# Scores of the delta-rule chunks without the masked-off half of the early queries, and one weight split per head pair moved to GpSimd

## The reference, cut to what matters

```python
def step(S, inp):
    r_t, w_t, k_t, v_t, aa_t, bb_t = inp
    sa = jnp.einsum('bhvk,bhk->bhv', S, aa_t)
    S = S * w_t[:, :, None, :] + sa[..., None] * bb_t[:, :, None, :] + v_t[..., None] * k_t[:, :, None, :]
    y_t = jnp.einsum('bhvk,bhk->bhv', S, r_t)
    return S, y_t
```

## Time and profile before

| | |
|---|---|
| three timed runs | 1025.52 us median, 1024.86 to 1025.6 |
| the profiled execution | 1025.08 us, its span 1023.1 us |
| TensorE busy | 1010.8 us (99%) |
| DVE busy | 736.5 us (72%) |
| ScalarE busy | 516.5 us (50%) |
| GpSimd busy | 218.1 us (21%) |
| where the changed stages lie | 214 to 540 us of the span |

### The profile page before, as it was taken

The page is one execution under the profiler, slowest core; times in us unless marked ns, Lnnn a source line. Parts: engine busy times, 40 slices in busy tenths (PEclk is TensorE's granted clock), DMA queues, the critical chain, the costliest instruction groups (busy, mean ns, idle before and its releaser), DMA issues.

```text
span 1023.1 us, 18706 instructions
## 1 busy us (share of the span) xinstructions
PE 1010.8 (99%) x7098; PEld 806.0 (79%) x7098; DVE 736.5 (72%) x1233; ACT 516.5 (50%) x869; POOL 218.1 (21%) x290
## 2 busy tenths in 40 slices
PE   8999999999999999999999999999999999999997
PEld 7888888777777777777777888888888888888886
DVE  5224667788988988888877455367777777789786
ACT  6435766844445445345453322265455444467744
POOL 8532356230221312313210454000000000000000
PEclk9999999999999999999999999999999999999999
DMA  7874465331303313214356877613333333337653
GB/s 201 240 218 139 130 215 203 92 77 42 87 24 73 87 63 86 56 63 119 95 161 149 242 233 255 204 37 102 88 103 90 96 101 103 90 115 221 207 186 117
DMA packets 161291, 133.25 MB, mean 130 GB/s; under 512 B 32730, under 2 KB 137736, under 8 KB 161224
## 3 DMA queue, kind: packets, MB, share of 16 engines
q1 hardware_dynamic: 147552, 88.37, 29.8%
q0 software_dynamic: 13520, 43.90, 13.9%
q10 hardware_dynamic: 151, 0.04, 0.0%
HBM read 111.83 MB, written 20.45 MB: 129 GB/s over the span
## 4 chain that ended last, share of the span: by engine, by line
PE 94%; DVE 2%; ACT 1%; issue 1%; DMA 1%; POOL 0%; ACTq 0%; POOLq 0%; DVEq 0%
PE ps L2075 15%; PE ps L2078 14%; PE ps L2077 14%; PE ps L2031 6%; PE ps L2033 5%; PE ps L2032 5%; PE ps L2634 3%; PE ps L2632 3%; PE ps L2633 3%; PE ps L2247 3%; PE ps L2380 2%; PE ps L2188 2%; PE ps L2567 1%; PE ps L2568 1%; PE ps L2566 1%; PE ps L2329 1%
## 5 line engine op out<-in xcount | busy, mean ns | idle before, releaser
L1340 DVE TENSOR_TENSOR wlo<-raw,whi 128x1024 fp32r<-128x1024 f32 x106 | 138.8, 1310 | 131.6 <-ACT whi L874 113.7
L874 ACT ACTIVATE whi<-raw 128x1024 fp32r<-128x1024 f32 x116 | 122.6, 1057 | 129.7 <-PE ps L2078 117.6
L2075 PE MATMUL ps<-xnh,whi 128*128 128x512 f32 x336 | 130.7, 389 | 0.0
L2077 PE MATMUL ps<-xnl,whi 128*128 128x512 f32 x336 | 130.7, 389 | 0.0
L2078 PE MATMUL ps<-xnh,wlo 128*128 128x512 f32 x336 | 130.7, 389 | 0.0
L2075 PE MATMUL ps<-xh,whi 128*128 128x512 f32 x232 | 91.5, 394 | 1.0 <-DVE xl L1358 1.0
L2077 PE MATMUL ps<-xl,whi 128*128 128x512 f32 x232 | 90.4, 390 | 0.0
L2078 PE MATMUL ps<-xh,wlo 128*128 128x512 f32 x232 | 90.3, 389 | 0.0
L2031 PE MATMUL ps<-xh,whi 128*128 128x512 f32 x192 | 89.5, 466 | 0.0
L2033 PE MATMUL ps<-xh,wlo 128*128 128x512 f32 x192 | 76.0, 396 | 0.0
L2032 PE MATMUL ps<-xl,whi 128*128 128x512 f32 x192 | 75.3, 392 | 0.0
(11 more groups left out here) (424 smaller groups left out, 2434.4 us busy)
## 6 DMA issues: line engine op xcount, KB each, us to landing
raw<-in_w_in SPq DMA_DIRECT2D x108, 256.0 KB, 3.2
raw<-in_w_up SPq DMA_DIRECT2D x88, 256.0 KB, 3.0
wrow<-in_w_down POOLq DMA_DIRECT2D x22, 512.0 KB, 5.3
raw<-weight_scratch SPq DMA_DIRECT2D x44, 256.0 KB, 3.4
raw<-in_w_down SPq DMA_DIRECT2D x32, 256.0 KB, 3.0
weight_scratch<-wrow POOLq DMA_DIRECT2D x11, 512.0 KB, 3.1
gates_scratch<-gst POOLq DMA_DIRECT2D x16, 256.0 KB, 3.3
raw<-in_w_proj_b SPq DMA_DIRECT2D x16, 256.0 KB, 4.0
```

The source lines that it names most:

```text
L874: act.activation(flat(whi[:, hb]), flat(raw[:, b]), ACT.Copy).then_inc(w_hi, 1)
L1340: dve.tensor_tensor(flat(lo[:, hb]), flat(raw[:, b]), flat(hi[:, hb]).bitcast(F32), ALU.subtract).then_inc(w_lo, 1)
L2075: pe.matmul(ps[bank][:, :], whi[:, hb, k, :], hi(k), start=first and k == 0, stop=False)
L2077: pe.matmul(ps[bank][:, :], whi[:, hb, k, :], lo(k), start=False, stop=False)
```

## The change

- The score matmuls are split by query. *Late* queries (64 to 127 of a chunk) keep all 128 keys: 8 matmuls per source, over 2 x 64 columns (a and r), all four chunks of a head in one bank (`LATE_BANK`). *Early* queries (0 to 63) are multiplied by the first 64 keys alone, since the others are masked off: for each source, chunk and head one matmul on 64 rows by 64 columns; chunks alternate (`e`) between the lower and the upper partition half of a bank, and both sources share the bank of a head (`EARLY_BANK`). The order is late for `bp`, early for both, late for `kp`. The wait for a free bank in the middle (`f == 6`) is gone.
- `gb` and `gk` lie next to each other as one tile `gg`, so that one masked copy moves the early scores of both. DVE's masks are still 8 per pair: two late ones for `gb`, four early ones of 64 partitions (from either PSUM half to partitions 0 to 63), then, behind the deviations, two late ones for `gk`. All of `gb` is complete after six masks, and ScalarE's `score_copy` waits for six instead of four. The transposes of z, `bp` and `kp` wait for one, two and six masks instead of three, four and eight. The early masks of pair 0 wait for the clearing of `gk`.
- DVE's `weights(N_FILL + 3 * n)` between scan and masks is gone; GpSimd does it as `low_weights`, first in its turn for pair n; DVE waits for it before the next half of weights (`w_lo`).

```diff
-SCORE_BANK = (0, 1, 2, 3, 4, 5, 0, 1)
+LATE_BANK = ((2, 3), (4, 5))
+EARLY_BANK = (0, 1)
...
-        gb = take("gb", [P, NT, 2, 2 * C])
+        gg = take("gg", [P, NT, 2, 2, 2, C])
+        gb, gk = (gg[:, 2 * i:2 * i + 2].rearrange("p x e h q t -> p (x e) h (q t)")
+                  for i in range(2))
...
-        gk = take("gk", [P, NT, 2, 2 * C])
...
+            def low_weights(n):
+
+                pool.wait_ge(w_hi, n + 1)
+                pool.wait_ge(w_lo, n)
+                pool.tensor_tensor(flat(wlo[:, n % HL]), flat(raw[:, slot(n)]),
+                                   flat(whi[:, n % HL]).bitcast(F32), ALU.subtract).then_inc(w_lo, 1)
...
+                low_weights(N_FILL + 3 * n)
                 bonus_product(n)
...
-                act.wait_ge(g_ready, n * 8 + 4)
+                act.wait_ge(g_ready, n * 8 + 6)
...
+            def two_parts(t, ts):
+                return t.rearrange("p (q t) -> p q t", q=2)[:, :, ts]
+
+            def predicated(dst, mask, scores, f):
+                dve.memset(carrier[:, f:f + 1], 0.0)
+                dve.copy_predicated(dst, mask.bitcast(U32).unsqueeze(1)
+                                    .to_broadcast([mask.shape[0], NT, 2, C // 2]), scores)\
+                    .then_inc(g_ready, 1)
+
+            def late_masked(n, i, h):
+                f = 6 * i + h
+                if n == 0:
+                    dve.wait_ge(cleared, 1 + i)
+                dve.wait_ge(g_ps, n * 8 + f + 1)
+                predicated((gb, gk)[i][:, :, h, :].rearrange("p j (q t) -> p j q t", q=2)
+                           [:, :, :, C // 2:], two_parts(causal[:, :], slice(C // 2, C)),
+                           ps[LATE_BANK[i][h]][:, :].rearrange("p (j q t) -> p j q t", j=NT, q=2), f)
+
+            def early_masked(n, h, e):
+                if n == 0:
+                    dve.wait_ge(cleared, 2)
+                dve.wait_ge(g_ps, n * 8 + 6)
+                predicated(gg[0:HD, :, e, h, :, 0:C // 2],
+                           two_parts(causal[0:HD, :], slice(0, C // 2)),
+                           ps[EARLY_BANK[h]][e * HD:(e + 1) * HD, :]
+                           .rearrange("p (x q t) -> p x q t", x=NT, q=2), 2 + 2 * h + e)
+
+            def masked(n, i):
+                if i:
+                    late_masked(n, 1, i - 1)
+                    return
+                for h in range(2):
+                    late_masked(n, 0, h)
+                for h in range(2):
+                    for e in range(2):
+                        early_masked(n, h, e)
...
+                        if lv == 1 and n:
+                            dve.wait_ge(w_lo, N_FILL + 3 * n + 1)
                         weights_half(N_FILL + 3 * n + 1, lv - 1)
...
-                weights(N_FILL + 3 * n)
                 fill_low(3 * n - 1)
-                for f in range(6):
-                    masked(n, f)
+                masked(n, 0)
                 deviations(n - 1)
-                for f in range(6, 8):
-                    masked(n, f)
+                for i in range(1, 3):
+                    masked(n, i)
...
+                def late(i):
+                    src = (bp, kp)[i]
+                    for j in range(NT):
+                        for h, hs in enumerate(rows):
+                            ins = pe.matmul(ps[LATE_BANK[i][h]][:, j * C:(j + 1) * C]
+                                            .rearrange("p (q t) -> p q t", q=2),
+                                            src[hs, j * C:(j + 1) * C], both(hs, j, slice(HD, C)),
+                                            start=True, stop=True)
+                            if j == NT - 1:
                                 ins.then_inc(g_ps, 1)
+
+                late(0)
+                for i, src in enumerate((bp, kp)):
+                    for jj in range(2):
+                        o = (2 * i + jj) * C
+                        for e in range(2):
+                            j = 2 * jj + e
+                            for h, hs in enumerate(rows):
+                                ins = pe.matmul(ps[EARLY_BANK[h]][e * HD:(e + 1) * HD, o:o + C]
+                                                .rearrange("p (q t) -> p q t", q=2),
+                                                src[hs, j * C:j * C + HD], both(hs, j, slice(0, HD)),
+                                                start=True, stop=True)
+                                if i and jj:
+                                    ins.then_inc(g_ps, 1)
+                late(1)
...
-                pe.wait_ge(g_ready, n * 8 + 3)
+                pe.wait_ge(g_ready, n * 8 + 1)
                 turned(2, z[:, n + 16, :]).then_inc(tok_ps, 1)
-                pe.wait_ge(g_ready, n * 8 + 4)
+                pe.wait_ge(g_ready, n * 8 + 2)
                 turned(3, bp).then_inc(tok_ps, 1)
...
-                pe.wait_ge(g_ready, n * 8 + 8)
+                pe.wait_ge(g_ready, n * 8 + 6)
                 turned(1, kp).then_inc(tok_ps, 1)
```

More of the change, by code:

```diff
@@ L1502, in deviations @@
                 spread(ysq, ystd).then_inc(vex_ready, 1)
-            def masked(n, f):
-                j0, h = (f % 4) // 2 * 2, f % 2
-                dst = (gb, gk)[f // 4][:, j0:j0 + 2, h, :]
+            def two_parts(t, ts):
[7 more added lines that the diff above has]
+                f = 6 * i + h
                 if n == 0:
-                    dve.wait_ge(cleared, 1 + f // 4)
+                    dve.wait_ge(cleared, 1 + i)
                 dve.wait_ge(g_ps, n * 8 + f + 1)
[L1512 to L1516, removed]
+                predicated((gb, gk)[i][:, :, h, :].rearrange("p j (q t) -> p j q t", q=2)
[18 more added lines that the diff above has]
+                        early_masked(n, h, e)
             def add_bonus(d):
@@ L1701, in _ @@
             weights(n + 2)
-            for f in range(8):
-                masked(0, f)
+            for i in range(3):
+                masked(0, i)
             value_tokens(0)
@@ L2239, in scores, with both @@
                     pe.wait_ge(ps_free, N_FILL - 1)
[L2240 to L2249, removed]
+                rows = [slice(h * HD, (h + 1) * HD) for h in range(2)]
+                def both(hs, j, ts):
+                    return ar[hs, 1 - n % 2, j, :].rearrange("p (q t) -> p q t", q=2)[:, :, ts]
+                def late(i):
[5 more added lines that the diff above has]
+                                            src[hs, j * C:(j + 1) * C], both(hs, j, slice(HD, C)),
                                             start=True, stop=True)
-                            if j > j0:
+                            if j == NT - 1:
                                 ins.then_inc(g_ps, 1)
+                late(0)
[12 more added lines that the diff above has]
+                late(1)
                 if d is not None:
```

## The result

The change makes the kernel slower: 1030.34 us (median of 6 runs, 1029.88 to 1030.87) against 1025.28 (6 runs, 1024.86 to 1025.6), ratio 1.0052, 95% interval 1.0042 to 1.0063. That is 5.06 us more, where 2.9 more was forecast (1028.4, range 1023.7 to 1032). The profiled execution took 1029.88 us, its span 1028.1.

The account below looks back on a forecast made before the run. TensorE, with 94% of the chain that ended last, was taken to bound the kernel. 2.9 (scan) + 1.4 (pair 0) - 1.4 (pairs 1 to 7) = 2.9 on the median 1025.52 gave 1028.4 us, range 1023.7 to 1032.

Parts of the forecast that it names:

- main mechanism: Scan: GpSimd's 2.4 us weights hold kmod to 1.4 us, stm queues behind it, TensorE goes on 0.41 us late.
- rival C: Scan: kmod doesn't wait for GpSimd, saving 2.9 us; 1025.5 with masks at 0.73; chance 0.17.
- The block at 59.15: Earlier trace: DVE's weights beside a GpSimd operation took 2.75 us instead of 1.22; used to predict kmod's delay.
- Scores: TensorE's score stage in each pair: 3.23 us instead of 3.66, early quarters four at once, variance sums 0.43 earlier.
- rival D: Score stage: quarters run two at once, deviations come 0.65 us later in each pair, 1033 us; chance 0.13.
- The masks' pace: DVE's early masks in each pair: 0.73 us apart, no overlap, because each turns the read side to other partitions.
- the rival with overlap: DVE's early masks keep their overlap, 0.63 us apart, giving 1025.6 us; chance 0.22.
- They neither gain nor lose: DVE's deviations, pair 3: six masks end at 342.03, deviations start at 342.01 now, so their start stays the same.
- the term of pairs 1 to 7: Gain of 0.12 us in each of pairs 3 to 7 and 0.4 in pairs 1 and 2: 1.4 us.
- If that cover were gone, it would be those tenths: Inversion: later n2 may set DVE's first product back some tenths, covered by filler; otherwise those tenths are lost per pair.
- Pair 0: Early masks wait for the clearing of gk, delaying n1, n2 and yy; TensorE's level-1 products end about 1.4 us later.
- The largest term, the scans: Seven scans, each 0.41 us late on TensorE with nothing to give it back: 2.9 us added.

Follow-up runs that it names:

- half order: Changed kernel with the four early masks reordered, both heads of the lower PSUM half, then both of the upper: 1028.22 us, ratio 1.0031.
- The run with the product placed: Changed kernel with half order, later kmod, pair 0's gb masks first, bonus store before n2, bonus product waiting for DVE's second-level low weights: 1024.04 us.
- Pair 0's run: Changed kernel with pair 0's early masks split by destination, gb's four before the clearing of gk, gk's four after: 1029.61 us, ratio 1.0046.

## Why the prediction was right, and where it was off

- **Direction and main mechanism: right.** GpSimd's weights took 2.36 us (forecast 2.4), kmod 1.35 (1.4), TensorE's delay 0.39 per scan (0.41), 2.90 in all (2.9). Moving kmod alone gives 2.15 us back, which rules out rival C. The block at 59.15, seen on another form of instruction, carried over to kmod's. The runs show it on three kinds of DVE instruction, each with two SBUF inputs: kmod 1.35 for 0.68, DVE's low weights 1.10 for 0.68, the 16-bit xx 1.24 for 0.69.
- **Scores: right.** 3.22 us (forecast 3.23), four quarters at once; rival D is out.
- **The masks' pace: the rival with overlap is out, the size was short.** My 0.73 was an estimate, since no row of before has a change of half, and I took an overlap of zero as the worst case; it measured 0.75 to 0.78, since the next mask starts only 0.03 to 0.05 after the end of the last. "They neither gain nor lose" was the step of the sum that was mis-sized: the deviations come 0.2 later, and the term of pairs 1 to 7 is -0.51 and not -1.4. The half order puts the price of a change of half at 0.14 us (0.77 for 0.63).
- **The late bonus product: not foreseen, 1.1 us.** "If that cover were gone, it would be those tenths" looked at n2's users on DVE alone. Behind n2 in GpSimd's queue stand the bonus store and its return, and at the end of that chain DVE's ysb, whose slack in pairs 1 and 2 was 2.2 us. The step named what is queued behind n1 on ScalarE, and not what is queued behind n2 on GpSimd. The run with the product placed shows the chain: with the store ahead, the cost in both pairs is gone. But n2 is the smaller part. It made the store 0.7 us late, inside the slack; the store's landing added 1.5, and why is open. In pair 1 the return starts 4.0 us after the store instead of 2.5, with the DMA engines busy for 7% of that time in both kernels, and 3.4 to 4.4 in every run with the changed scores and the store behind n2; in pairs 3 to 7 it is mostly 2.1, and no run isolates the cause.
- **Pair 0: right, 1.43 for 1.4.** The delay of n1, n2 and yy was as forecast (yy's second half used at 226.20, forecast 226.3). From filler to filler only 1.05 shows, since TensorE's wait ahead of the scores, which the change doesn't touch, is 0.38 shorter in this trace. Pair 0's run shows that without the wait for the clearing DVE's masks and vp would be 0.4 behind.
- The forecast's remaining error is then: -0.35 (the wait ahead of pair 0), +0.9 (masks), +1.1 (bonus), +0.4 (small delays in the inversions, unassigned), in all 2.0 of the 2.2 us by which the medians' difference of 5.06 lies above the forecast 2.9. The largest term, the scans, was exact; the masks' term and the missing bonus product are 2.0 us together.

Where the expected gain went: TensorE saves 0.44 us of scores per pair and DVE takes it back at once, because its masks are still eight of 512 elements in each partition, and four of them make it change halves. With every repair (the product placed) it is still no more than 0.9 us of 1025, which the interval doesn't tell from nothing.

## What to carry to other kernels

Less matmul work ahead of a drain that stayed the same size only moved the wait here (0.44 us gained at the scores of a pair, 0.64 lost ahead of its deviations): count the drain's instructions, their pace and what is queued behind them first. GpSimd's instructions beside the tight DVE chain needed a window free of DVE instructions with two SBUF inputs (beside one, kmod took 1.35 us for 0.68, while stm, with one input in PSUM, kept its 0.35), and that window has an edge on both sides: making one earlier (the store first, 1.7 us more) or later (the deviations between the masks, 10.8 us more) cost more than the wait that it removed. Of a delayed instruction, follow its own queue to the last reader, DMAs included, and in every pair: the same store landed after 2.1 us in most pairs and after 3.6 and 4.0 in two.

## What the runs showed of the hardware that was not expected

- The delay at a change of partition half shows on the tiny reciprocal behind the masks too (0.77 from the last mask's start), and no overlap with the mask before was left: in pair 3 of the changed kernel each instruction behind a change started 0.03 to 0.04 us after the end of the one before.
- The DVE instructions of 0.68 us that GpSimd held up ended 0.53 to 0.56 us after GpSimd's in all the traces, though they had started at different times behind it: kmod (1.55 behind its start) at 333.87 after 333.33, the low weights (0.73) at 355.14 after 354.60, xx (1.46 and 1.44) at 349.31 after 348.76 and at 352.45 after 351.90.
- It can be GpSimd that stands. Its product of 1.28 us took 1.70, 1.59, 1.55, 1.53, 1.37 and 1.35 us when DVE's low weights had started 0.12, 0.24, 0.27, 0.29, 0.46 and 0.48 us before it, and ended 1.14 us after them each time (pairs 1 and 2 of five kernels). The earlier trace rows has the other outcome: DVE's weights at 59.15 started 0.36 ahead of GpSimd's product and stood all the same; GpSimd was issuing a DMA just before (58.91 to 59.48), and no run separates the two cases.
- 16-bit data didn't escape it: xx, float16 with float16, took 1.21 to 1.25 beside n2 where it started 1.43 to 1.48 us behind it, and 0.68 or 0.69 where it started 2.03 or more behind.
- In pair 3 of the changed kernel the copy-predicated instructions on 64 partitions x 512 elements took 0.71 to 0.74 us, about as much as those on 128 partitions (0.71 to 0.75); on 64 x 256 elements, in pair 0's run, they took 0.43 to 0.46.
